# RMS factors applied to the results of two dense products, tokens turned unscaled in quarters, with a new layer front and new routing arithmetic

## The chip, the cores and the metric

The kernel runs on 1 core of one Trainium2 chip. The metric is the device time of one execution in microseconds (us), lower is better.

## The reference

256 tokens of width 1024 go through two blocks. Cut to what matters here:

```python
def hybrid_layer(x, ...):                                  # block 1, one layer
    z = rms_norm(x, g_mix) @ w_in
    ...
    merged = gt[:, :, 0] * (o_a @ p_a) + gt[:, :, 1] * (o_b @ p_b) + gt[:, :, 2] * (o_c @ p_c)
    x = x + merged @ w_out
    u = rms_norm(x, g_ffn) @ w_gu                          # 1024 -> 2 x 2816
    gate, up = jnp.split(u, 2, axis=-1)
    return x + (jax.nn.silu(gate) * up) @ w_down

def first_block(x, ...):
    ...
    return rms_norm(x, g_final)

def second_block(x, w_in, ...):                            # two layers
    for l in range(DEPTH_2):
        h = jnp.einsum('bsd,dc->bsc', x, w_in[l])
        a_q, a_k, a_v, b_q, b_k, b_v, i_q, i_k, i_w, c_q, c_kv, c_kr = split_cols(h)
        o_a = sliding_window_sink_attn(...)
        o_b = indexer_sparse_attn(...)                     # top 64 keys by sum_h w_idx * relu(q_idx k_idx)
        q_c = rms_norm_2(c_q, c_q_norm_g[l]) @ w_uq[l]
        kv_c = rms_norm_2(c_kv, c_kv_norm_g[l]) @ w_ukv[l]
        o_c = mla_attn(...)
        x = layer_norm(DEEPNORM_ALPHA * x + mix @ w_out[l], ln1_g[l], ln1_b[l])
        x = layer_norm(DEEPNORM_ALPHA * x + moe_ffn(x, ...), ln2_g[l], ln2_b[l])

def moe_ffn(x, ...):                                       # 16 experts in 4 groups
    scores = jax.nn.sigmoid(xt @ w_router)
    biased = (scores + router_bias).reshape(N, N_GROUPS, EXPERTS_PER_GROUP)
    group_score = jnp.sum(lax.top_k(biased, TOP_K)[0], axis=-1)
    g_sel = jnp.argmax(group_score, axis=-1)
    in_group = jnp.take_along_axis(biased, g_sel[:, None, None], axis=1)[:, 0]
    _, local = lax.top_k(in_group, TOP_K)
    ...
```

## The kernel before

**Data.** The tokens lie in `x_tok[128, t, 1024]` (t = 0, 1, 128 tokens each). For a product they are turned to `act_hi`/`act_lo` (`act_both`): 8 tiles k of 128 columns by 256 tokens. Every product is made from split operands: a number is rounded to a short form (hi) and its rest (lo), and three matmuls hi·hi, hi·lo, lo·hi stand for one (`three`, L966 to L968; in an FFN tile `both_tile`, L1106 to L1110, where hi and lo of the tokens are one 512-column operand). Weights come by DMA into `raw` in tiles of 128x2048; ScalarE writes their hi half `whi` (`split_hi`, L1757), VectorE their rest `wlo` (`split_lo`, L2194), and tile n lies in slot n % 3 of each. Five engine programs are written out by hand, one after the other, and semaphores tie them: the order of the code is the order of each engine.

**Dense part.** After w_out (4 tiles from number `T_WO`, each a `down_tile` of 24 matmuls) comes the FFN norm, then 11 FFN steps (`experts`): gate tile, up tile, w_down tile, from number `T_FFN` = 40. Of each step VectorE sums the two halves of gate and up (L2422), ScalarE makes silu (L1952), VectorE the product (L2442), ScalarE and VectorE its hi and lo. The norms before the FFN and after it (`g_final`) are one function each side: VectorE adds the product to x (`add`, L2386), ScalarE sums squares (L1808), GpSimd raises to the power -1/2 (L839), VectorE makes a diagonal matrix of the factors (`diag2`, L2395), TensorE turns and scales in one matmul x_tok · diag2 (`turn_scaled`, L1093), ScalarE and VectorE apply the gain by column while they round (L1815, L2410). While that runs TensorE does `keep_warm` matmuls (L1045), whose results nobody reads. The first tile is taken up column tile by column tile (`first_tile`).

**Layers of block 2.** `L_PAIRS` are column groups of w_in_2 that are made token half by token half, each from two weight tiles: pair 0 holds the indexer's columns, pair 1 those of the two low-rank vectors c_q and c_kv, pair 2 the window attention's queries. Then come two single column tiles (`columns`), the low-rank products (`up_queries`, `up_keys`), and the turned queries and keys. The indexer: GpSimd rotates its queries and keys (rope, L906 to L909, copies L917), TensorE turns them (L1352) and multiplies (L1411), ScalarE takes relu (L2047, L2048), VectorE sums the heads (L2532), strikes out the 64 largest in 8 rounds (L2539, L2540) and writes the mask (L2557, L2559). Weight splits lie between the rounds. After the mask the attention units begin with `logits` (L2223). The mean squares of c_q and c_kv are VectorE's (`norm_stats`, L2492 to L2496), the power GpSimd's (L930), the scaling VectorE's (L2521).

**Routing.** After the first layer norm TensorE turns the tokens, multiplies with the router (L1483), ScalarE makes exp (L2108), and VectorE finds each token's group out of 4 by pairwise comparison (L2636 to L2665, semaphore `one_ready`). TensorE counts tokens of each group (L1543 to L1546), VectorE orders the groups (L2668 to L2672, `ord_ready`; SyncE reads that order and issues the experts' weights, L743) and makes a 0/1 matrix of places (L2683, `put_ready`) with which TensorE gathers the tokens (L1558, L1559). `xt_hi`/`xt_lo` (L2105, L2629) are the split tokens it gathers from. `keep_warm` stands in TensorE's two waits.

In the profile before, `arena`, `small` and `pbuf` are the buffers from which the smaller tiles are carved.

## Time and profile before

| | |
|---|---|
| median of 3 runs | 1106.47 us (1105.86 to 1106.81) |
| the profiled execution | 1107.15 us, its span 1105.4 us |
| mean granted TensorE clock | 0.997 |
| TensorE busy | 1069.6 us, 97 % of the span |
| VectorE busy | 739.3 us, 67 % |
| ScalarE busy | 546.2 us, 49 % |
| GpSimd busy | 107.8 us, 10 % |

Times in the rows are us from the start of the span. A timeline row gives start, length, engine, line, operation, tiles, and in brackets the idle time before it with what ended it. A matmul's length contains its way through the array (0.39 us for 512 columns, though the next begins 0.23 us later), so lengths of matmuls are read from start to start.

### The profile page before, as it was taken

What the parts mean: (1) busy time and instruction counts of PE and PEld (TensorE: products, weight loads), DVE (VectorE), ACT (ScalarE), POOL (GpSimd) and SP (SyncE); (2) the same over time, 40 slices, a digit from 0 to 9 for tenths busy, and PEclk for the clock granted to TensorE, in tenths of its full rate; (3) what the DMA queues carried; (4) which work ended last, traced back from release to release, by engine and by line L of the source; (5) the groups of instructions that cost most, each with busy time, mean ns of one, the idle gap of its engine ahead of it and who ended that gap; (6) DMA issues with size and microseconds to landing.
All of it is one profiled execution on the core that took longest, in us unless ns stands there. A gap on an engine that the chain in (4) does not pass through costs nothing.

```text
span 1105.4 us, 15299 instructions
## 1 busy us (share of the span) xinstructions
PE 1069.6 (97%) x5828; PEld 872.7 (79%) x5828; DVE 739.3 (67%) x984; ACT 546.2 (49%) x728; POOL 107.8 (10%) x159
## 2 busy tenths in 40 slices
PE   8999999999999999999899999999998999999996
PEld 8899987888888888888787766777787877667765
DVE  5544635687576666659978745886879768357856
ACT  5344455673444444454753434664356625245741
POOL 3000020100000000015600000000067000000000
PEclk9999999999999999999999999999999999999998
DMA  9763443544465555534311878987344017789971
GB/s 293 222 207 115 127 157 128 180 165 151 152 219 194 192 180 195 186 116 134 114 61 39 312 277 337 369 322 265 119 141 150 5 49 274 271 319 374 348 266 39
DMA packets 107759, 214.59 MB, mean 194 GB/s; under 512 B 6834, under 2 KB 52042, under 8 KB 107696
## 3 DMA queue, kind: packets, MB, share of 16 engines
q1 hardware_dynamic: 105072, 209.38, 54.6%
q0 software_dynamic: 1312, 3.88, 1.1%
q8 instruction: 41, 0.67, 0.3%
q10 hardware_dynamic: 1312, 0.49, 0.2%
q14 instruction: 22, 0.18, 0.0%
HBM read 212.63 MB, written 1.09 MB: 193 GB/s over the span
## 4 chain that ended last, share of the span: by engine, by line
PE 75%; DVE 14%; ACT 4%; DMA 3%; issue 2%; POOL 1%; SPq 1%; ACTq 0%; DVEq 0%
PE ps L966 15%; PE ps L968 14%; PE ps L967 14%; PE ps L1107 7%; DVE wlo L2194 3%; PE ps L1106 3%; PE ps L1071 3%; PE ps L1622 2%; PE ps L1002 2%; PE ps L1004 2%; PE ps L1003 2%; ACT whi L1757 2%; DMA arena<-in_w_down 2%; PE ps L1037 2%; PE ps L1056 1%
## 5 line engine op out<-in xcount | busy, mean ns | idle before, releaser
L2194 DVE TENSOR_TENSOR wlo<-raw,whi 128x2048 fp32r<-128x2048 f32 (+4 forms) x145 | 316.0, 2181 | 180.7 <-ACT whi L1757 180.0
L1757 ACT ACTIVATE whi<-raw 128x2048 fp32r<-128x2048 f32 (+4 forms) x145 | 261.7, 1808 | 174.3 <-PE ps L968 71.7
L966 PE MATMUL ps<-whi,act_both 128*128 128x512 f32 (+2 forms) x416 | 155.4, 373 | 4.8 <-DVE wlo L2194 4.2
L968 PE MATMUL ps<-whi,act_both 128*128 128x512 f32 (+2 forms) x416 | 151.7, 365 | 0.0
L967 PE MATMUL ps<-wlo,act_both 128*128 128x512 f32 (+2 forms) x416 | 151.6, 364 | 0.0
L1107 PE MATMUL ps<-act_both,whi 128*128 128x512 f32 x344 | 119.1, 396 | 0.6 <-DVE wlo L2194 0.6
L2194 DVE TENSOR_TENSOR wlo<-arena,whi 128x2048 fp32r<-128x2048 f32 (+1 forms) x36 | 75.9, 2113 | 39.1 <-ACT whi L1757 39.0
L966 PE MATMUL ps<-whi,mix_hi 128*128 128x512 f32 (+1 forms) x244 | 96.0, 394 | 1.3 <-DVE mix_lo L2568 0.5
L966 PEld LDWEIGHTS ps<-whi,act_both 128*128 128x128 f32 x416 | 78.4, 188 | 22.9 <-issue 7.6
L968 PE MATMUL ps<-whi,mix_lo 128*128 128x512 f32 (+1 forms) x244 | 95.0, 389 | 0.0
L967 PE MATMUL ps<-wlo,mix_hi 128*128 128x512 f32 (+1 forms) x244 | 94.8, 389 | 0.0
L968 PEld LDWEIGHTS ps<-whi,act_both 128*128 128x128 f32 x416 | 78.4, 188 | 12.4
L967 PEld LDWEIGHTS ps<-wlo,act_both 128*128 128x128 f32 x416 | 78.5, 189 | 10.9
L1757 ACT ACTIVATE whi<-arena 128x2048 fp32r<-128x2048 f32 (+1 forms) x36 | 64.1, 1781 | 45.7 <-DMA arena<-in_w_up 24.7
L1106 PE MATMUL ps<-act_both,wlo 128*128 128x256 f32 x301 | 83.9, 279 | 0.0
L839 POOL TENSOR_TENSOR small<-small 128x1 f32<-128x1 f32 x14 | 8.2, 587 | 769.8 <-DVE small L2206 488.5
L1107 PEld LDWEIGHTS ps<-act_both,whi 128*128 128x128 f32 x344 | 62.2, 188 | 12.9 <-issue 0.9
L966 PE MATMUL ps<-act_both,whi 128*128 128x256 f32 x216 | 62.0, 287 | 0.0
L967 PE MATMUL ps<-act_both,whi 128*128 128x256 f32 x216 | 61.1, 283 | 0.0
L968 PE MATMUL ps<-act_both,wlo 128*128 128x256 f32 x216 | 61.1, 283 | 0.0
L1106 PEld LDWEIGHTS ps<-act_both,wlo 128*128 128x128 f32 x301 | 56.8, 189 | 1.9
L966 PEld LDWEIGHTS ps<-whi,mix_hi 128*128 128x128 f32 x244 | 45.8, 188 | 13.5 <-issue 2.9
(329 smaller groups left out, 1934.3 us busy)
## 6 DMA issues: line engine op xcount, KB each, us to landing
raw<-in_w_in SPq DMA_DIRECT2D x43, 1024.0 KB, 5.4
raw<-in_w_down SPq DMA_DIRECT2D x23, 1024.0 KB, 5.2
raw<-in_w_gu SPq DMA_DIRECT2D x22, 1024.0 KB, 5.1
raw<-in_w_out SPq DMA_DIRECT2D x12, 1024.0 KB, 4.9
raw<-in_w_gate SPq DMA_DIRECT2D x24, 512.0 KB, 5.6
raw<-in_w_up SPq DMA_DIRECT2D x24, 512.0 KB, 6.6
arena<-in_w_gate SPq DMA_DIRECT2D x20, 512.0 KB, 5.1
arena<-in_w_up SPq DMA_DIRECT2D x20, 512.0 KB, 6.2
```

What stands on the lines that cost most here:

```text
L966: pe.matmul(o, ah, bh, start=first, stop=False)
L967: pe.matmul(o, ah, bl, start=False, stop=False)
L968: return pe.matmul(o, al, bh, start=False, stop=last)
L1002: pe.matmul(o, a, cc, start=f, stop=False)
L1003: pe.matmul(o, a, d, start=False, stop=False)
L1004: x = pe.matmul(o, b, cc, start=False, stop=g)
L1037: x = pe.matmul(o[:, i, :], u["q"][i], u["k"][i], start=True, stop=True)
L1071: x = pe.matmul(oo, pt[:, b * P:(b + 1) * P], u["v"][i][kt], start=f, stop=g)
L1106: pe.matmul(ps[:, bank + part, 0:256], wl[:, k, m], act_hi[:, k, :], start=False, stop=False)
L1107: x = pe.matmul(ps[:, bank + part, :].rearrange("p (a b) -> p a b", a=2), wh[:, k, m], act_both[:, k, :, :], start=k == 0, stop=k == KD - 1)
L1757: act.activation(whi[:, c % 3, 0:n], raw_of(c, v)[:, 0:n], ACT.Copy).then_inc(hi_made, 1)
L2194: dve.tensor_tensor(wlo[:, c % 3, 0:n], raw_of(c, v)[:, 0:n], whi[:, c % 3, 0:n].bitcast(F32), ALU.subtract)\
```

## The change

**Both dense norms.** x is turned as it is, in four quarters (`turn_early`: four transposes of 128x128), between the parts of the last w_out tile, of the first gate tile (`first_gate`), of the last w_down tile and of layer 0's first columns. ScalarE (`early_rounded`) and VectorE (`remainders`) apply only the gain by column. The factor rstd of each token is applied afterwards: in the FFN to the gate sums (`normed`, one VectorE multiply of 128x512 in each of 11 steps with `rstd_rows`, a tile that TensorE and VectorE make once), to the result of w_down where it is added to x, and in layer 0 as the scale of the evacuations. (The up sums are left unscaled, since the factor comes in at that addition.) `turn_scaled` and the two `keep_warm(0, 6)` are gone; ScalarE's splits of the second FFN step stand ahead of the first silu.

**Layer front, both layers.** The indexer's rope is VectorE's (`idx_rope`), its turns and products on TensorE stand ahead in the order, the mean squares and the scaling of c_q and c_kv are ScalarE's (`c_squares`), the addition of eps GpSimd's, their gains are applied by column when the turned values are split (three narrow operations each on ScalarE and VectorE), and weight splits 6 to 9 and the strike rounds are regrouped on VectorE.

**Routing, both layers.** Fewer VectorE operations between exp and the orders and places, counts and keys multiplied by 4, the key made by a matmul on a constant, `max_index` in place of copy and mask; half of `xt_lo` moved behind `put_ready`; the second `xt_hi` moved behind exp; the router's second half for t = 0 moved behind the turn of t = 1; `keep_warm` 2 to 0, 12 to 6 and 10 to 6.

```diff
+                rows(0, 0).then_inc(early_out, 1)
+                rows(0, 1).then_inc(early_out, 1)
+                turn_early(last, 0, 0)
+                rows(1, 0).then_inc(early_out, 1)
+                turn_early(last, 0, 1)
+                if last == 1:
+                    rows(1, 1, (0,))
+                    turn_early(last, 1, 0)
+                    rows(1, 1, (1,)).then_inc(tile_used, 1)
+                else:
+                    rows(1, 1).then_inc(tile_used, 1)
+            def turn_early(nth, t, half):
+                pe.wait_ge(x_added, 4 * nth - 4 + 2 * t + half + 1)
+                for k in range(4 * half, 4 * half + 4):
+                    x = pe.transpose(early_at(t, k), x_tok[:, t, k * P:(k + 1) * P], ident)
+                x.then_inc(early_full, 1)
...
-                for k in range(KD):
-                    o = turned_at(k, slice(t * P, (t + 1) * P), apart)
-                    x = pe.matmul(o, x_tok[:, t, k * P:(k + 1) * P], diag2[:, t, :], start=True, stop=True)
...
+                rounded(0)
+                turn_early(1, 1, 1)
+                rounded(1)
...
+                        for t in range(TT):
+                            pe.wait_ge(diag_set, TT + t + 1)
+                            x = pe.matmul(ps[:, 4, t * P:(t + 1) * P], cst[:, C_FOUR:C_FOUR + P], diag2[:, t, :], start=True, stop=True)
+                        x.then_inc(rows_full, 1)
+                        both_tile(c + 1, v, 2, (1,))
...
-                    keep_warm(0, 6)
-                    for t in range(TT):
-                        pe.wait_ge(diag_set, 2 * TT + t + 1)
-                        turn_scaled(t, True, True)
...
+                            elif half == 0:
+                                turn_early(2, 1, 0)
+                                turn_early(2, 1, 1)
...
-                for half in range(2):
-                    for t in range(TT):
-                        pair_columns(1, half, t)
-                pe.wait_ge(rope_done, l * 5 + 1)
+                pair_columns(1, 0, 0)
+                pair_columns(1, 0, 1)
+                pe.wait_ge(idx_turned, l + 1)
                 turns(pairs(IQ, 2) + doubled(0))
-                pair_columns(2, 0, 0)
+                pair_columns(1, 1, 0)
                 tb_wait(1)
...
-                for half in range(2):
-                    pe.wait_ge(tr_lo, l * 12 + 5 + half)
-                    route(0, half, (0, 1, 2))
+                pe.wait_ge(tr_lo, l * 12 + 5)
+                route(0, 0, (0, 1, 2))
                 keep_warm(5, 4)
                 turn(x_tok, 1, l * 8, True)
-                keep_warm(5, 2)
+                pe.wait_ge(tr_lo, l * 12 + 6)
+                route(0, 1, (0, 1, 2))
                 for half in range(2):
...
-                keep_warm(7, 12)
+                keep_warm(7, 6)
...
-                keep_warm(7, 10)
+                keep_warm(7, 6)
...
+            def early_rounded(nth, t):
+                for half in range(2):
+                    act.wait_ge(early_full, 4 * nth - 4 + 2 * t + half + 1)
+                    for k in range(4 * half, 4 * half + 4):
+                        act.activation(act_hi[:, k, t * P:(t + 1) * P], early_at(t, k), ACT.Copy,
+                                       scale=g_col[:, nth * KD + k:nth * KD + k + 1]).then_inc(early_hi, 1)
...
+                def c_squares(t):
+                    for q, (c0, n) in enumerate(((CQ, C_QR), (CKV, C_KVR))):
+                        x = act.activation(c_squared[q], h[:, t, c0:c0 + n], ACT.Square, scale=n ** -0.5,
+                                           accum_out=cvar[:, 2 * t + q:2 * t + q + 1])
+                    return x
...
+                    if nth == 1:
+                        dve.tensor_tensor(x, x, o, ALU.add).then_inc(x_added, 1)
+                    else:
+                        dve.scalar_tensor_tensor(out=x, in0=o, scalar=rstd[:, t:t + 1], in1=x, op0=ALU.mult, op1=ALU.add).then_inc(x_added, 1)
+                def remainders(t, half):
+                    for k in range(4 * half, 4 * half + 4):
+                        dve.wait_ge(early_hi, 2 * KD * (nth - 1) + KD * t + early_shared(t, k) + 1)
+                        m = slice(t * P, (t + 1) * P)
+                        dve.scalar_tensor_tensor(out=act_lo[:, k, m], in0=early_at(t, k), scalar=g_col[:, nth * KD + k:nth * KD + k + 1],
+                                                 in1=act_hi[:, k, m].bitcast(F32), op0=ALU.mult, op1=ALU.subtract).then_inc(early_lo, 1)
...
+                def normed(e):
+                    dve.wait_ge(gate_sum, e + 1)
+                    g = f_gate.rearrange("p (a b) -> p a b", a=2)
+                    dve.tensor_tensor(g, g, spread(rstd_rows, 1, 2), ALU.mult).then_inc(gate_ready, 1)
...
+                    dve.tensor_tensor(a3, x, c3, ALU.mult)
+                    dve.tensor_tensor(b3[:, :, 0:32], x[:, :, 32:64], s_lo, ALU.mult)
+                    lk(dve.tensor_tensor(b3[:, :, 32:64], x[:, :, 0:32], s_hi, ALU.mult))
+                    lk(dve.tensor_tensor(x, a3, b3, ALU.add))
...
+                dve.tensor_copy(key_sb, keys)
+                lk(dve.max(sorted_key, keys))
+                dve.max_index(vec8, sorted_key, key_sb).then_inc(ord_ready, 1)
```

TensorE at the end of w_out and the start of the FFN, before: the six fillers, sixteen scaled turns, then the first gate tile.

```order
L1045 MATMUL ps<-mix_hi 128x512 x6
L1093 MATMUL ps<-arena,x_tok 128x128 x16
L1123 MATMUL ps<-act_both,whi 128x256 x8
L1126 MATMUL ps<-act_both,wlo 128x256 x8
L1130 MATMUL ps<-act_both,whi 128x256 x8
```

The same place of the change (L971 to L973 are w_out's last tile, L1029 the transposes, L1160 and L1161 `first_gate`):

```order
L973 MATMUL ps<-whi,act_both 128x512
L1029 MATMUL ps<-cst,x_tok 128x128 x4
L971 MATMUL ps<-whi,act_both 128x512
L972 MATMUL ps<-wlo,act_both 128x512
L973 MATMUL ps<-whi,act_both 128x512
L1029 MATMUL ps<-cst,x_tok 128x128 x4
L971 MATMUL ps<-whi,act_both 128x512
L972 MATMUL ps<-wlo,act_both 128x512
L973 MATMUL ps<-whi,act_both 128x512
L1160 MATMUL ps<-act_both,whi 128x256
L1161 MATMUL ps<-act_both,wlo 128x256
```

Fillers and scaled turns are gone, and turns stand among the products.

VectorE in a layer's front, before: the last of four norm statistics, the indexer's weights (L2513), a weight split, the scaling of c_q and c_kv, then the indexer's sums (L2532).

```order
L2492 BN_STATS small<-arena 128x6
L2493 BN_AGGR small<-small 128x2
L2494 SCALAR_TENSOR_TENSOR small<-small 128x1
L2496 TENSOR_SCALAR small<-small 128x1
L2513 TENSOR_SCALAR small<-arena 128x4 x2
L2515 TENSOR_SCALAR small<-small 128x8
L2194 TENSOR_TENSOR wlo<-raw,whi 128x768
L2521 SCALAR_TENSOR_TENSOR arena<-arena,small 128x256
L2521 SCALAR_TENSOR_TENSOR arena<-arena,small 128x128
L2521 SCALAR_TENSOR_TENSOR arena<-arena,small 128x256
L2521 SCALAR_TENSOR_TENSOR arena<-arena,small 128x128
L2532 SCALAR_TENSOR_TENSOR arena<-pbuf,small,cst 128x256
```

The same place of the change (L2270 is `split_lo`, L2589 to L2600 the indexer's rope, L2615 its sums):

```order
L2270 TENSOR_TENSOR wlo<-raw,whi 128x1424
L2589 TENSOR_TENSOR arena<-arena,cst 128x320
L2590 TENSOR_TENSOR arena<-arena,cst 128x5x32
L2591 TENSOR_TENSOR arena<-arena,cst 128x5x32
L2592 TENSOR_TENSOR arena<-arena 128x320
L2599 COPY arena<-arena 128x128
L2600 COPY arena<-arena 128x128
L2270 TENSOR_TENSOR wlo<-raw,whi 128x2048 x2
L2606 TENSOR_SCALAR small<-arena 128x4 x2
L2608 TENSOR_SCALAR small<-small 128x8
L2615 SCALAR_TENSOR_TENSOR arena<-pbuf,small,cst 128x256
```

Statistics, scaling and the 768-column split no longer stand ahead of the sums; the rope does, among the splits.

VectorE in the routing, before, from the end of the group comparison to the places:

```order
L2650 TENSOR_TENSOR arena<-arena 128x32
L2653 TENSOR_REDUCE arena<-arena 128x8
L2665 TENSOR_SCALAR arena<-arena 128x8
L2629 TENSOR_TENSOR mix_lo<-x_tok,mix_hi 128x512
L2668 SCALAR_TENSOR_TENSOR arena<-ps,cst 128x8
L2670 MAX arena<-arena 128x8
L2671 CAST arena<-arena 128x8
L2672 TENSOR_SCALAR arena<-arena 128x8
L2674 TENSOR_TENSOR arena<-arena 128x16
L2675 TENSOR_REDUCE arena<-arena 128x4
L2676 SCALAR_TENSOR_TENSOR arena<-arena 128x4
L2678 SCALAR_TENSOR_TENSOR arena<-arena,ps 128x8
```

The same place of the change:

```order
L2730 TENSOR_TENSOR arena<-arena,cst 128x32
L2733 TENSOR_REDUCE arena<-arena 128x8
L2713 TENSOR_TENSOR mix_lo<-x_tok,mix_hi 128x512
L2747 COPY arena<-ps 128x8
L2748 MAX arena<-ps 128x8
L2749 MAX_INDEX arena<-arena 128x8
L2750 TENSOR_TENSOR arena<-arena 128x16
L2751 TENSOR_REDUCE arena<-arena 128x4
L2753 SCALAR_TENSOR_TENSOR arena<-arena,ps 128x8
```

Three operations of this piece are gone, and `MAX_INDEX` is new; ahead of it, 11 operations between the biased scores and `one_ready` (L2658 to L2665) have become 8.

## Rows read from the trace of the kernel before

**Rows 1.** The page: busy time, share of the span, instructions of TensorE

```profile
PE 1069.6 (97%) x5828; PEld 872.7 (79%) x5828; DVE 739.3 (67%) x984; ACT 546.2 (49%) x728; POOL 107.8 (10%) x159
```

**Rows 2.** Windows: length, busy PE, PEld, DVE, ACT, POOL, PEclk, DMA share, GB/s

```profile
306.00:472.00 166.00, 165.92 (x879) 142.30 (x880) 111.33 (x74) 68.68 (x51) 0.00 (x0) 1.00 0.59 194
...
495.00:540.00 45.00, 42.70 (x272) 37.40 (x272) 39.57 (x96) 26.41 (x31) 31.31 (x47) 1.00 0.43 139
...
595.00:617.00 22.00, 18.91 (x134) 15.74 (x133) 19.32 (x51) 9.74 (x14) 0.55 (x1) 1.00 0.36 109
```

**Rows 3.** Timeline of TensorE from w_out to the second FFN step

```profile
286.53 1.52 PE L1045 MATMUL ps<-mix_hi 128*128 128x512 f32 x6
288.96 3.84 PE L1093 MATMUL ps<-arena,x_tok 128*128 128x128 f32 x32 [0.92 <-DVE arena L2395]
292.56 1.01 PE L1123 MATMUL ps<-act_both,whi 128*128 128x256 f32 x3
...
306.08 0.47 PE L1107 MATMUL ps<-act_both,whi 128*128 128x512 f32 x1 [0.61 <-DVE wlo L2194]
```

**Rows 4.** Timeline of VectorE in the last FFN steps

```profile
451.79 0.69 DVE L2442 TENSOR_TENSOR arena<-arena 128x512 f32<-128x512 f32 x1
...
463.57 2.29 DVE L2194 TENSOR_TENSOR wlo<-raw,whi 128x2048 fp32r<-128x2048 f32 x1 [0.79 <-ACT whi L1757]
```

**Rows 5.** Timeline of TensorE from w_down to pair 1 of layer 0

```profile
477.84 1.52 PE L1045 MATMUL ps<-mix_hi 128*128 128x512 f32 x6
...
483.85 0.48 PE L966 MATMUL ps<-whi,act_both 128*128 128x512 f32 x1
...
494.87 0.32 PE L966 MATMUL ps<-whi,act_both 128*128 128x356 f32 x1
```

**Rows 6.** Timeline of VectorE in layer 0's front

```profile
503.39 0.43 DVE L2492 BATCH_NORM_STATS2 small<-arena 128x6 f32<-128x256 f32 x1
...
508.82 1.41 DVE L2521 SCALAR_TENSOR_TENSOR arena<-arena,small 128x256 f32<-128x256 f32 x4
510.15 0.86 DVE L2532 SCALAR_TENSOR_TENSOR arena<-pbuf,small,cst 128x256 f32<-128x256 f32 x2
...
537.39 0.68 DVE L2223 SCALAR_TENSOR_TENSOR pbuf<-ps,cst 128x512 f32<-128x512 f32 x1
```

**Rows 7.** Timeline of ScalarE in layer 0's front

```profile
495.07 0.60 ACT L2012 ACTIVATE arena<-ps 128x512 f32<-128x512 f32 x1 [1.26 <-PE ps L968]
...
499.03 1.92 ACT L1757 ACTIVATE whi<-raw 128x2048 fp32r<-128x2048 f32 x1 [1.57 <-PE ps L968]
...
507.81 1.03 ACT L2047 ACTIVATE pbuf<-ps 128x1024 f32<-128x1024 f32 x1 [2.96 <-PE ps L1411]
```

**Rows 8.** Timelines of layer 1's front: TensorE (pair 1 begins), VectorE (first logits)

```profile
802.76 0.32 PE L966 MATMUL ps<-whi,act_both 128*128 128x356 f32 x1
...
846.52 0.68 DVE L2223 SCALAR_TENSOR_TENSOR pbuf<-ps,cst 128x512 f32<-128x512 f32 x1
```

**Rows 9.** Waits of TensorE: released by; us in total, times, longest us

```profile
PE ps L966 <- DVE wlo L2194: 4.5, 6, 1.8
```

**Rows 10.** Timeline of GpSimd in layer 0's front

```profile
495.81 0.89 POOL L906 TENSOR_TENSOR arena<-arena,cst 128x320 f32<-128x320 f32 x1 [2.63 <-ACT arena L2012]
...
497.75 2.80 POOL L909 TENSOR_TENSOR arena<-arena 128x320 f32<-128x320 f32 x1
```

**Rows 11.** Timelines of layer 0's routing: ScalarE, VectorE, SyncE's queue

```profile
602.55 2.08 ACT L2105 ACTIVATE mix_hi<-x_tok 128x1024 fp32r<-128x1024 f32 x1
...
603.29 1.98 DVE L2629 TENSOR_TENSOR mix_lo<-x_tok,mix_hi 128x1024 fp32r<-128x1024 f32 x1
...
609.54 0.17 DVE L2672 TENSOR_SCALAR arena<-arena 128x8 int32<-128x8 int32 x1
...
610.95 0.75 DVE L2683 TENSOR_SCALAR moe_r<-cst,arena 128x384 fp32r<-128x384 f32 x2
...
610.75 0.35 SPq L743 DMA_DIRECT2D raw<-in_w_gate  x1
```

More of the change, by code:

```diff
@@ L604, in apart, with early_at, early_shared @@
                 eng.wait_ge(semaphore, awaited)
-        def turned_at(k, m, apart):
-            if apart and m.start:
-                return ps[:, 6 + k // 4, (k % 4) * P:(k % 4 + 1) * P]
-            return ps[:, 2 + k // 2, (k % 2) * S + m.start:(k % 2) * S + m.stop]
+        def early_at(t, k):
+            bank = EARLY_BANK[t][k]
+            c = EARLY_BANK[t][:k].count(bank) * P
+            return ps[:, bank, c:c + P]
+        def early_shared(t, k):
+            return max(x for x in range(KD) if EARLY_BANK[t][x] == EARLY_BANK[t][k])
         def unit_first(u):
@@ L987, in cols_tile, with down_tile @@
                     last.then_inc(tile_used, 1)
-            def down_tile(c, v, hi, lo, first, last):
+            def down_tile(c, v, hi, lo, first, last=0):
                 tile_ready(c, v)
@@ L994, in down_tile, with rows @@
                 wl = wlo[:, s, :].rearrange("p (k c) -> p k c", k=2)
-                for t in range(TT):
-                    for half in range(2):
-                        for k in range(2):
-                            m, n = slice(t * P, (t + 1) * P), slice(half * 512, half * 512 + 512)
-                            o = ps[:, 4 + 2 * t + half, :]
-                            f, g = first and k == 0, last and k == 1
-                            a, b, cc, d = hi[:, k, m], lo[:, k, m], wh[:, k, n], wl[:, k, n]
-                            pe.matmul(o, a, cc, start=f, stop=False)
-                            pe.matmul(o, a, d, start=False, stop=False)
-                            x = pe.matmul(o, b, cc, start=False, stop=g)
-                        if last and not (t and half):
-                            x.then_inc(early_out, 1)
-                x.then_inc(tile_used, 1)
+                def rows(t, half, ks=(0, 1)):
+                    m, n = slice(t * P, (t + 1) * P), slice(half * 512, half * 512 + 512)
+                    for k in ks:
+                        x = three(ps[:, 4 + 2 * t + half, :], hi[:, k, m], lo[:, k, m], wh[:, k, n], wl[:, k, n],
+                                  first and k == 0, last > 0 and k == 1)
+                    return x
+                if not last:
+                    for t in range(TT):
+                        for half in range(2):
+                            x = rows(t, half)
+                    x.then_inc(tile_used, 1)
+                    return
+                rows(0, 0).then_inc(early_out, 1)
[14 more added lines that the diff above has]
+                x.then_inc(early_full, 1)
             def turn(src, t, before, by_four=False, first_bank=0, halves=(0, 1)):
@@ L1125, in first_tile @@
                 for k in range(KD):
-                    pe.matmul(o, wl[:, k, m], act_hi[:, k, :], start=False, stop=apart and k == KD - 1)
+                    pe.matmul(o, wl[:, k, m], act_hi[:, k, :], start=False, stop=False)
                 for k in range(KD):
                     if k % 2 == 0:
-                        pe.wait_ge(k_lo, pairs + k // 2 + 1)
-                    pe.matmul(ps[:, 0, 256:512] if apart else o, wh[:, k, m], act_lo[:, k, :], start=apart and k == 0, stop=k == KD - 1)
@@ L2378, in _, with early_sums @@
                                       act_hi[:, 4 * half:4 * half + 4, :].bitcast(F32), ALU.subtract).then_inc(m_lo, 1)
-            for n in range(T_WO + 2, T_FFN + 2):
+            for n in range(T_WO + 2, T_FFN + 1):
                 split_lo(n)
-            def add_and_factor(used, nth):
+            def early_sums(used, nth, rest):
                 def add(t, half):
@@ L2448, in experts @@
                 gate(0, c0, v0)
+                for t in range(TT):
+                    dve.wait_ge(rstd_ready, TT + t + 1)
+                    dve.tensor_scalar(diag2[:, t, :], ident, rstd[:, t:t + 1], 0.25, ALU.mult, ALU.mult).then_inc(diag_set, 1)
                 split_lo(c0 + 2, v0)
+                dve.wait_ge(rows_full, 1)
+                dve.tensor_copy(rstd_rows, ps[:, 4, 0:S]).then_inc(rows_set, 1)
+                dve.wait_ge(rows_set, 1)
+                normed(0)
                 product(0, c0 + 1, v0)
@@ L2618, in layer @@
                     else:
-                        for part in range(2):
-                            turned_lo_half(l * 3 + 1, 0, part)
+                        turned_lo_half(l * 3 + 1, 0, 0)
                     dve.wait_ge(gln_in, l * 64 + 32)
@@ L2684, in layer @@
                 ins.then_inc(put_ready, 1)
-                rest_of(1, slice(1, 2))
-                dve.tensor_scalar(inside, pos, float(S), None, ALU.is_lt)
-                beaten(flat(bi), 8)
-                ranks(8, cnt8)
+                for t in range(TT):
+                    rest_of(t, slice(1, 2))
+                dve.tensor_scalar(inside, pos, 4.0 * S, None, ALU.is_lt)
+                beaten(flat(bi), 8, ALU.is_gt)
+                lk(over(8, cnt8, ALU.add))
                 def gates():
```

346 lines of the change are left out of this document (179 added, 167 removed).

## The prediction, written before the change was run

> **What bounds the kernel.** I read the page first: TensorE is busy for 97 % of the span [rows 1]. The windows by stage say where the missing 3 % lie: an FFN step has none (165.9 us busy in 166), while a layer's front (42.7 of 45 us) and a routing (18.9 of 22) do, and the clock is granted in full in all of them [rows 2]. But busy is not useful: the timelines show filler matmuls, and the stretches from the last product before a norm to the first one behind it, which no busy share reveals [rows 3, 5]. So the time is that of TensorE's useful matmuls plus such stretches, and only what shortens a stretch counts. In a front VectorE is the other bound: 39.6 us busy of 45 [rows 2], and the first `logits` wait for its chain of sums, strikes and mask [rows 6].
>
> **FFN entry.** w_out's last matmul gives way to the fillers at 286.53; the first gate matmul starts at 292.56, the second step's gate at 306.08 [rows 3]. That is 19.55 us. What useful work lies in it? From 306.08 to the fillers at 477.84 [rows 3, 5] lie ten steps and one w_down tile. A matmul of 512 columns takes 0.227 us from one to the next (six fillers in 1.52 us, less one way through the array), a w_down tile of 24 therefore 5.45; so a step takes (171.76 - 5.45)/10 = 16.63, and gate plus up 11.18. The change needs besides: 16 transposes at 0.112 each (the 32 passes of L1093 take 3.6 us up to the gate matmul; I take a transpose as one pass) = 1.8, and two matmuls for `rstd_rows`, 0.45. 13.4 in all, a gain of 6.1. I take off 0.5 for waits: turned quarters must be added, rounded and given their remainders in time, and the fourth is turned only 0.9 us after w_out's end while VectorE still has four remainders and an addition of 0.7 us to do. **5.6 us.** ScalarE's reordered splits should take the wait of 0.61 for `wlo` away; its cover is the up tile.
>
> **FFN steps.** `normed` adds one 128x512 multiply per step, 0.69 us by its like, L2442 [rows 4], and silu waits for it. VectorE is busy 111.3 of 166 us [rows 2], 11.1 of 16.6 per step, and behind the gate sum it stands idle for 0.79 us until the next split is ready [rows 4]: the multiply fits there. What is late next is silu, by 0.7 us; the hidden values are used a whole tile later (5.6 us). I cost it at nothing; with the cover gone it is at most 11 times 0.69, 7.6 us.
>
> **Layer 0 entry.** Fillers begin at 477.84, pair 0 at 483.85 [rows 5]: 6.0 us. The change puts 1.8 us of transposes there: 4.2, of which I keep **4.1 us**. The scaled evacuations replace unscaled ones of the same size; the two more at the single columns lie beside TensorE's work.
>
> What do both entries do to the clock? It was granted in full where TensorE waited in a routing for 3 of 22 us [rows 2], so I cost the new mixture at nothing. A rule speaks against that. The Trainium skill, "TensorE: Matmul & The Clock Gate", Part 4, says that a transpose does not count as TensorE's busy time for the clock, and the change puts transposes where fillers and real matmuls stood. By that rule the clock could be low behind each entry; no row here shows transposes at a fallen clock. What it would cost I work out as rival 3, from rows.
>
> **Layer fronts.** Count from X, the end of pair 0 (494.87 [rows 5], 802.76 [rows 8]). Before, layer 0's sums start at X+15.3 and logits at X+42.5 [rows 6]; layer 1's logits at X+43.8 [rows 8]. Removed from VectorE ahead of the sums are the four statistics (from 503.39, 4.1 us) and the scaling (1.41) [rows 6]; added are two ropes, 1.6 us each by 128x512 at 0.69 scaled to 320 columns with their fixed part, which fall mostly in waits for ScalarE's splits. Now ScalarE decides: behind X it has an evacuation (0.60), split 4 (1.92), the turned queries, split 5, an evacuation, two squares, and relu (1.03 and a half of that) [rows 7], about 9 us of work and 1.7 of waits for TensorE: sums at X+10.7, 4.6 earlier. Given back: split 6 (0.96 us, 768 columns at the rate of the others) moves behind them, and the remainder of the low-rank vectors is three operations instead of one (+0.4): 3.2 by VectorE's way. ScalarE's way to the first exp gives some 2.2. I take **2.8 us** in layer 0 and, since layer 1 is 1.3 us slower at the same point and loses that to a rope wait and a `wlo` wait of the same chain, **3.9 us** there. The largest wait of TensorE for `wlo`, 1.8 us [rows 9], should go too, but it is no further gain: logits wait for VectorE.
>
> One row speaks against the move: on GpSimd a rope's last addition, 320 columns, took 2.80 us while VectorE made a split, and its first multiply of that width 0.89 us while VectorE stood idle [rows 10]. If the hold is mutual, VectorE's new ropes pay for it too; but the two engines' ropes now lie apart in time, and GpSimd's statistic and small ropes beside them take 0.2 to 0.3 us a piece, so I cost it at nothing, at most 1 us per layer.
>
> **Routing, each layer.** Before: `xt_lo` holds VectorE from 603.29 for 1.98 us, `xt_hi` ScalarE to 604.6, and exp waits for that; the order is ready at 609.7, SyncE issues weights at 610.75, the places are written from 610.95 [rows 11]. Removed: half of `xt_lo` ahead of the comparison (0.9, of which I count 0.8, the exp behind `xt_hi` coming earlier too), three small operations at 0.17 to 0.2 ahead of `one_ready` (0.5), one in the ordering and one in the places (0.4). Added: `max_index`, which no row shows; nearest are operations of 0.17 on 8 columns [rows 11], so from 0.17 to twice that. Gather and weights shift together: **1.7 us**, twice, 3.4. The fillers taken out here (14 of 24) leave TensorE idle instead, at no cost but the clock's.
>
> **Sum.** 5.6 + 4.1 + 2.8 + 3.9 + 3.4 = 19.8 us, 1.8 %. The profiled execution took 1107.15, so 1087.35; the median of the runs stands 0.68 under it: **1086.7 us**. A measurement tells 0.2 %, 2.2 us, from no change.
>
> **The rivals.**
> 1. *The fronts give nothing*: ScalarE, with squares, scalings and three narrow roundings more, is late for relu or the first exp. For it: it decides already by my count. Against: 26.4 busy of 45 us [rows 2]. 1086.7 + 6.7 = 1093.4. Chance 0.13.
> 2. *The entries give half*: TensorE waits at each quarter for addition, rounding, remainder. For it: each quarter passes three engines; against, half a tile of matmuls lies between. 1086.7 + 4.9 = 1091.6. Chance 0.08.
> 3. *The clock falls* from 2.4 to 1.2 GHz, in the thinned routings or behind the entries. Against: a wait of 1.8 us [rows 9] and routings with waits had it at 1.00 [rows 2]. One tile of 5.6 us at half speed behind each entry adds 11.2: 1097.9; the 5 us between places and the end of a routing [rows 2, 11], twice, 1096.7. Say 1097. Chance 0.04.
> 4. *It does not do what it says*: the stretches stay, held by something unseen: 1106.5. Chance 0.02.
> 5. *Slower*: the FFN step becomes a chain (gate sum, `normed`, silu, product, hidden split, w_down) longer than TensorE's 16.63. It must exceed it by 2.0 us in ten steps to eat 19.8; at 3 us the time is 1086.7 + 30 = 1117. For it: one operation more in that chain, between two splits of 2.29 us that can hold VectorE. Against: a third of VectorE's step is idle. Chance 0.03.
>
> The forecast itself has 0.70; its own range is 1083.5 to 1090.5 (transposes and waits at nothing, layer 0's front at 3.2, layer 1's at 4.3, against `max_index` at twice, waits doubled and 2.2 for layer 0). To leave out no more than 2 in 10 the range goes from 1082 to 1094.5, over rivals 1 and 2. Faster 0.95, same 0.02, slower 0.03.
>
> **What would show it.** In the profile after: no matmul L1045 at the norms; the first gate matmul at about 288 and the second step's at 300.5; 16.6 us per FFN step as before; pair 0 begins right behind w_down; X to logits about 39.7 us in both layers, with VectorE without idle before them; the order to SyncE about 1.7 us earlier after the router; PEclk at 1.00 everywhere. Wrong would be: gaps of over 0.5 us at L1160 or L1029; FFN steps over 16.7 us; logits released by ScalarE; a low clock in a routing.

## The result

The change is faster, by 1.35 %: 1091.78 us median of 4 executions (1089.31 to 1094.59) against 1106.64 of before, a ratio of 0.9865 with a 95 % interval from 0.9846 to 0.9883. The forecast was 1086.7, with a range from 1082 to 1094.5: the sign is right, the gain is 14.9 us where 19.8 were forecast. The profiled execution took 1093.08 us, its span 1091.3.

The page of the changed kernel; its third row is the TensorE clock in 40 slices, in tenths:

```profile
PE 1060.8 (97%) x5768; PEld 865.7 (79%) x5768; DVE 744.5 (68%) x976; ACT 554.5 (51%) x766; POOL 93.5 (9%) x141
...
PEclk9999999999999999999899999999999999999998
```

TensorE is as busy as before by share [rows 1]; in us its busy time is 8.8 less. One slice in the middle has an 8; before no stretch of the kernel's middle had one. It comes back below.

Timeline of TensorE in the changed kernel, from w_out's last matmul over the turn between the first gate's parts to the second FFN step (the second matmul of the 300.02 row), then layer 0's entry and the first matmul of pair 1 in each layer:

```profile
287.79 0.40 PE L973 MATMUL ps<-whi,act_both 128*128 128x512 f32 x1
288.05 0.35 PE L1160 MATMUL ps<-act_both,whi 128*128 128x256 f32 x1
...
300.02 0.62 PE L1122 MATMUL ps<-act_both,whi 128*128 128x512 f32 x2
...
475.63 1.03 PE L1029 MATMUL ps<-cst,x_tok 128*128 128x128 f32 x8
...
484.70 0.32 PE L971 MATMUL ps<-whi,act_both 128*128 128x356 f32 x1
...
793.61 0.32 PE L971 MATMUL ps<-whi,act_both 128*128 128x356 f32 x1
```

The gate follows w_out after 0.26 us, and the second step starts at 300.25 instead of 306.08 [rows 3]: 5.8 us. Pair 1 starts at 484.70 instead of 494.87 [rows 5], 10.2 earlier, so layer 0's entry gave 4.3. Eight transposes take 0.79 us from start to start, 0.1 each.

Timeline of VectorE in an FFN step of the changed kernel (L2517 is `normed`), then its first logits in layers 0 and 1:

```profile
455.69 1.23 DVE L2503 TENSOR_REDUCE arena<-ps 128x512 f32<-128x1024 f32 x1 [0.77 <-PE ps L1122]
456.95 0.69 DVE L2517 TENSOR_TENSOR arena<-arena 128x512 f32<-128x512 f32 x1
457.70 2.29 DVE L2270 TENSOR_TENSOR wlo<-raw,whi 128x2048 fp32r<-128x2048 f32 x1
...
525.91 0.69 DVE L2299 SCALAR_TENSOR_TENSOR pbuf<-ps,cst 128x512 f32<-128x512 f32 x1 [0.45 <-PE ps L1052]
...
834.52 0.69 DVE L2299 SCALAR_TENSOR_TENSOR pbuf<-ps,cst 128x512 f32<-128x512 f32 x1 [0.31 <-PE ps L1052]
```

The multiply stands exactly in the hole of [rows 4], and from the second to the last step the gate sums lie 16.48 us apart, against 16.54 before. The logits now come 41.2 us after X in layer 0 and 40.9 in layer 1, against 42.5 and 43.8 [rows 5 to 8]: gains of 1.3 and 2.9, and VectorE now waits just before them (0.45 and 0.31 us), which it did not.

The windows of the changed kernel around the slice with the lower clock (same columns as [rows 2]):

```profile
528.00:531.00 3.00, 2.55 (x16) 1.30 (x16) 2.90 (x6) 2.18 (x9) 2.84 (x5) 1.00 0.60 244
531.00:534.00 3.00, 2.00 (x13) 1.46 (x13) 2.86 (x6) 3.00 (x13) 2.10 (x5) 0.81 0.00 0
534.00:537.00 3.00, 3.00 (x18) 2.66 (x18) 1.13 (x7) 1.66 (x6) 0.00 (x0) 0.50 0.00 0
537.00:540.00 3.00, 3.00 (x16) 2.95 (x16) 1.70 (x4) 1.15 (x4) 0.00 (x0) 0.55 0.02 5
```

For some 7 us TensorE runs at 1.2 GHz, behind a stretch at the first attention units in which it was idle for 1.5 of 6 us. The last of these waits, 1.00 us for an evacuation by ScalarE (L2078), ends at 532.51, and the matmuls that start then are the first slow ones. The same wait stands at the same place in the trace of before, where the clock did not fall (TensorE):

```profile
543.91 0.64 PE L1352 MATMUL ps<-cst,arena 128*96 128x128 f32 x4 [1.00 <-ACT arena L2024]
```

Routing of layer 0 in the changed kernel: VectorE's order and places, SyncE's first weight issue, ScalarE's split waiting for the weights, the first expert product:

```profile
599.99 0.16 DVE L2749 FIND_INDEX8 arena<-arena 128x8 uint32<-128x8 f32 x1
...
601.06 0.75 DVE L2758 TENSOR_SCALAR moe_r<-cst,arena 128x384 fp32r<-128x384 f32 x2
...
601.19 0.35 SPq L749 DMA_DIRECT2D raw<-in_w_gate  x1
...
605.26 1.06 ACT L1805 ACTIVATE whi<-raw 128x1024 fp32r<-128x1024 f32 x1 [1.41 <-DMA raw<-in_w_up]
...
607.63 0.49 PE L971 MATMUL ps<-whi,act_both 128*128 128x512 f32 x1 [0.80 <-DVE wlo L2270]
```

The issue now comes 0.13 us behind the places; before, it came 0.20 ahead of them [rows 11]. The order gained less than the places, and the first expert product waits for the weights, which hang on the order.

### The profile page after: what moved, and what is told of

Same layout as the page of the kernel before. It is cut to its first block, busy times and chain, and to the rows that moved or that the text cites. A ratio compares the mean times of both kernels' runs of the same rounds, so it can differ in the third digit from the quotient of the medians.

```text
span 1091.3 us, 15196 instructions
## 1 busy us (share of the span) xinstructions
PE 1060.8 (97%) x5768; PEld 865.7 (79%) x5768; DVE 744.5 (68%) x976; ACT 554.5 (51%) x766; POOL 93.5 (9%) x141
## 4 chain that ended last, share of the span: by engine, by line
PE 85%; DVE 7%; POOL 3%; ACT 3%; issue 1%; DMA 1%; SPq 0%; ACTq 0%; DVEq 0%; POOLq 0%
PE ps L971 19%; PE ps L973 18%; PE ps L972 18%; PE ps L1122 7%; PE ps L1121 3%; PE ps L1094 3%; PE ps L1670 2%; PE ps L1060 2%; PE ps L1079 2%; PE ps L1692 1%; PE ps L1052 1%; DVE x_tok L2679 1%; ACT whi L1805 1%; DVE x_tok L2677 1%; POOL arena L915 1%
## 5 line engine op out<-in xcount | busy, mean ns | idle before, releaser
L2270 DVE TENSOR_TENSOR wlo<-raw,whi 128x2048 fp32r<-128x2048 f32 (+4 forms) x145 | 316.6, 2186 | 160.7 <-ACT whi L1805 160.0
L971 PE MATMUL ps<-whi,act_both 128*128 128x512 f32 (+2 forms) x448 | 168.2, 376 | 1.8 <-DVE wlo L2270 1.6
L973 PE MATMUL ps<-whi,act_both 128*128 128x512 f32 (+2 forms) x448 | 164.2, 367 | 0.0
L972 PE MATMUL ps<-wlo,act_both 128*128 128x512 f32 (+2 forms) x448 | 164.1, 366 | 0.0
L971 PE MATMUL ps<-whi,mix_hi 128*128 128x512 f32 x332 | 130.5, 393 | 1.4 <-DVE mix_lo L2652 0.5
L973 PE MATMUL ps<-whi,mix_lo 128*128 128x512 f32 x332 | 129.2, 389 | 0.0
L972 PE MATMUL ps<-wlo,mix_hi 128*128 128x512 f32 x332 | 129.1, 389 | 0.0
L971 PEld LDWEIGHTS ps<-whi,act_both 128*128 128x128 f32 x448 | 84.4, 188 | 20.7 <-issue 5.4
L2270 DVE TENSOR_TENSOR wlo<-arena,whi 128x2048 fp32r<-128x2048 f32 (+1 forms) x36 | 76.0, 2113 | 34.0 <-ACT whi L1805 34.0
L973 PEld LDWEIGHTS ps<-whi,act_both 128*128 128x128 f32 x448 | 84.4, 188 | 13.6
L1805 ACT ACTIVATE whi<-arena 128x2048 fp32r<-128x2048 f32 (+1 forms) x36 | 64.1, 1781 | 42.5 <-DMA arena<-in_w_up 25.1
L971 PEld LDWEIGHTS ps<-whi,mix_hi 128*128 128x128 f32 x332 | 62.3, 188 | 17.0 <-issue 4.1
L973 PEld LDWEIGHTS ps<-whi,mix_lo 128*128 128x128 f32 x332 | 62.3, 188 | 13.2
L972 PEld LDWEIGHTS ps<-wlo,mix_hi 128*128 128x128 f32 x332 | 62.4, 188 | 12.5
L971 PE MATMUL ps<-act_both,whi 128*128 128x256 f32 x216 | 62.0, 287 | 0.0
L973 PE MATMUL ps<-act_both,wlo 128*128 128x256 f32 x216 | 61.1, 283 | 0.0
```

The source lines that it names most:

```text
L971: pe.matmul(o, ah, bh, start=first, stop=False)
L972: pe.matmul(o, ah, bl, start=False, stop=False)
L973: return pe.matmul(o, al, bh, start=False, stop=last)
L1805: act.activation(whi[:, c % 3, 0:n], raw_of(c, v)[:, 0:n], ACT.Copy).then_inc(hi_made, 1)
L2270: dve.tensor_tensor(wlo[:, c % 3, 0:n], raw_of(c, v)[:, 0:n], whi[:, c % 3, 0:n].bitcast(F32), ALU.subtract)\
```

## The experiments

Each was run beside executions of before on the same chip. Over all these runs before took 1106.39 us in 37 of 48 executions at a mean clock of 0.997 or more (the median of these), and 1108.7 to 1110.4 in the other 11, at 0.994 or 0.995. Below, "full clock" means the executions at 0.997 or more.

**1. The three parts alone, and the change once more.** `dense_only`, `front_only` and `routing_only` are before with one group of the diff's hunks each; in `dense_only` the rows are made with ones and a factor of 1 instead of 4 and 0.25, since those constants belong to the routing.

```diff
-cst[:, C_FOUR:C_FOUR + P], diag2[:, t, :]
+cst[:, C_ONE:C_ONE + P], diag2[:, t, :]
-dve.tensor_scalar(diag2[:, t, :], ident, rstd[:, t:t + 1], 0.25, ALU.mult, ALU.mult)
+dve.tensor_scalar(diag2[:, t, :], ident, rstd[:, t:t + 1], None, ALU.mult)
```

> Only the two dense norms are changed; layer front and routing are those of before. Theory (the parts add up as the trace of the change shows them: 5.8 us at the FFN entry, 4.4 at layer 0's): 1106.6 - 10.2 = 1096.4 us, and the FFN steps stay at 16.6 us. Rival (the FFN steps give part of it back through the added multiply): over 1099 us.

> Only the layer fronts are changed. Theory (TensorE's own work becomes the bound at the first logits, so the front gives 1.3 us in layer 0 and 2.9 in layer 1, of which 0.7 is lost behind it): 1106.6 - 3.5 = 1103.1 us. If the clock falls in layer 0's attention units because of the new front, some executions stand 3.2 us above that. Rival (my prediction's sizes, 2.8 and 3.9): 1099.9 us.

> Only the routing is changed. Theory (1.6 us earlier at the places, but the first expert product only 1.2 and 1.4 earlier): 1106.6 - 2.6 = 1104.0 us. Rival (prediction: 1.7 each): 1103.2. Rival (fewer fillers bring the clock down): above 1106.

> The changed kernel, once more. Theory (a stretch of 7 us at 1.2 GHz at the start of layer 0's attention units in some executions, not in others): the times fall in two groups about 3 to 4 us apart, 1089 to 1090.5 with a mean clock of 0.997 or more, and 1093 to 1094.6 with 0.994. Rival (plain scatter): clocks and times unrelated.

| kernel | median, us | ratio, interval | full clock: median, executions | lower clock |
|---|---|---|---|---|
| dense_only | 1098.21 | 0.9917 [0.9894, 0.9941] | 1097.50, 3 of 4 | 1100.66 |
| front_only | 1104.05 | 0.9972 [0.9959, 0.9986] | 1103.24, 6 of 10 | 1105.4 to 1106.1 |
| routing_only | 1105.86 | 0.9991 [0.9980, 1.0003] | 1105.28, 7 of 10 | 1107.2 to 1107.4 |
| after_again | 1090.92 | 0.9864 [0.9840, 0.9888] | 1090.36, 3 of 5 | 1093.12, 1094.29 |

At full clock the parts give 8.9, 3.2 and 1.1 us, together 13.2, the whole 16.0. Two of the three theories for the parts were too high: `dense_only` by 1.3 us (10.2 were expected), `routing_only` by 1.5 (2.6). The parts are not additive: in the dense part alone the logits of layer 0 still hang on before's VectorE chain (the row has no wait ahead of it), and come 43.9 us after its pair 1 began, 1.4 later than before, so 1.4 of the 10 us won at the entries was given back there. Timelines of TensorE (pair 1) and VectorE (logits) in `dense_only`:

```profile
484.95 0.32 PE L974 MATMUL ps<-whi,act_both 128*128 128x356 f32 x1
...
528.87 0.68 DVE L2278 SCALAR_TENSOR_TENSOR pbuf<-ps,cst 128x512 f32<-128x512 f32 x1
```

The trace of `routing_only` shows the like in layer 1: the first expert product of layer 0 stands 2.2 us earlier than before (614.92 against 617.07), pair 1 of layer 1 1.4 (801.32), its first logits only 0.5. These are its rows of TensorE and VectorE:

```profile
801.32 0.32 PE L963 MATMUL ps<-whi,act_both 128*128 128x356 f32 x1
...
845.97 0.68 DVE L2224 SCALAR_TENSOR_TENSOR pbuf<-ps,cst 128x512 f32<-128x512 f32 x1
```

From pair 1 to the logits took 44.7 us there, 43.8 before. With the new front it takes 41 us in every trace but that of `pool_rope` (experiment 4). The two losses, 1.4 and 0.9 us, would make up most of the 2.8 by which the parts fall short of the whole; each is read from one execution. The front alone gave 3.2, as its theory said (3.5) and not as I predicted (6.7). The routing alone can't be told from nothing by its interval.

The changed kernel shows two groups, by time and clock together: over both sets five executions from 1089.3 to 1090.9 at full clock and four from 1093.1 to 1094.6 at 0.994 or 0.995. The plain-scatter rival falls: the profile of `after_again`, an execution at 0.997, has the same stretch without the fall.

```profile
531.00:534.00 3.00, 1.86 (x15) 1.30 (x15) 2.86 (x7) 2.88 (x10) 2.43 (x6) 1.00 0.00 0
534.00:537.00 3.00, 3.00 (x32) 2.81 (x30) 2.79 (x8) 2.90 (x11) 0.00 (x0) 1.00 0.02 5
```

The same order with the same idle time thus runs at either clock. Before has such executions too (11 of 48), and the lower group costs 3.1 us there, 3.3 here.

Where the clock fell is known only of profiled executions; of the change's four with a lowered clock that is one. The one profile of `dense_only` has the fall in layer 0's units, that of `front_only` in layer 1's, again right behind the wait of 1.00 us (TensorE, then the window):

```profile
849.20 0.77 PE L1352 MATMUL ps<-cst,arena 128*96 128x128 f32 x4 [1.00 <-ACT arena L2025]
...
852.00:855.00 3.00, 3.00 (x18) 2.62 (x18) 1.92 (x5) 2.00 (x7) 0.00 (x0) 0.50 0.00 0
```

**2. Fillers around the first units.** `no_fill` drops the fillers ahead of the first unit's products, `units_warm` adds six at units 2 and 3, `warm_nofill` does both, in both layers:

```diff
                 tb_wait(2)
-                keep_warm(3, 4)
...
+                    if i == 3:
+                        pe.wait_ge(pt_ready, nu + 1)
+                        keep_warm(2, 4)
                     late_turns(i)
+                    if i == 2:
+                        keep_warm(2, 2)
```

> The changed kernel with six more fillers in each layer's attention units (two at unit 2, four at unit 3 of each layer, where TensorE stands idle for 0.3 to 1.0 us). Theory (thin work at the first units lets the clock fall to 1.2 GHz in some executions, 3 to 4 us each): no execution with a mean clock under 0.996, all of them between 1089 and 1091.5. Rival (the fall comes from what stands ahead of the units, or from elsewhere): the upper group stays in about half of the executions, and the fillers cost up to 1 us.

> The changed kernel without the four fillers ahead of the first unit's products in each layer (0.9 us of TensorE). Theory (the first logits now wait for TensorE, by 0.45 and 0.31 us): 0.3 to 0.8 us less than the changed kernel in undisturbed executions, 1089.6 to 1090. Rival (VectorE is the bound): the same 1090.4. If thin work ahead of the units brings the clock down, falls become more frequent than 4 of 9.

> Both edits: no fillers ahead of the first unit, six more at units 2 and 3. Theory: the best of the set, 1089 to 1090.5 in all executions. Rival (the fillers ahead of the first unit hold the clock up): executions at 1093 and more remain.

`units_warm` 1093.62 (0.9874 [0.9856, 0.9893]), `no_fill` 1090.45 (0.9846 [0.9831, 0.9861]), `warm_nofill` 1093.86 (0.9869 [0.9850, 0.9887]). `units_warm` was a bad test, and its timeline of TensorE says why:

```profile
532.94 1.21 PE L1068 MATMUL ps<-mix_hi 128*128 128x512 f32 x4 [1.48 <-ACT pt L1840]
```

The fillers' bank had to be freed by ScalarE first, so they stood behind the idle time, made it longer (1.48 instead of 1.00 us) and delayed the units by 1.35 us in layer 0. Twice that is what its two executions at full clock lost (1092.92 and 1093.34 against 1090.36). The clock fell in the profiled execution too, in layer 1, and in that of `warm_nofill` in layer 0; two of four executions of each were at 0.994 to 0.996. So both theories missed, and whether fillers that wait for nothing guard the clock stayed open. `no_fill` saved nothing (full clock 1090.45 in 5 of 5, against 1090.36): my expectation that TensorE's amount of work delays the logits is wrong. No execution of it had a lowered clock. Its timelines of TensorE, ScalarE and VectorE:

```profile
524.08 0.38 PE L1397 MATMUL ps<-cst,arena 128*128 128x128 f32 x2
525.49 0.70 PE L1052 MATMUL ps<-arena 64*128 64x256 f32 x4 [1.03 <-ACT arena L2077]
...
524.28 0.84 ACT L2067 ACTIVATE arena<-ps,small 128x256 f32<-128x256 f32 x2 [2.25 <-PE ps L973]
525.00 0.39 ACT L2077 ACTIVATE arena<-ps 128x256 f32<-128x256 f32 x1
...
526.23 0.69 DVE L2298 SCALAR_TENSOR_TENSOR pbuf<-ps,cst 128x512 f32<-128x512 f32 x1 [0.49 <-PE ps L1052]
```

The chain is: second single column tile on TensorE, its evacuation on ScalarE (two scaled operations in layer 0, 0.84 us), then that of the last turned keys, then the first products, then the logits. Where the fillers stood, TensorE now waits for ScalarE.

**3. The cover of the added multiply.** `normed4` does it four times in each step, so the gate is scaled by the factor's fourth power.

```diff
+                    for i in range(3):
+                        dve.tensor_tensor(g, g, spread(rstd_rows, 1, 2), ALU.mult).then_inc(scaled_some, 1)
+                        dve.wait_ge(scaled_some, 3 * e + (i + 1))
                     dve.tensor_tensor(g, g, spread(rstd_rows, 1, 2), ALU.mult).then_inc(gate_ready, 1)
```

> The changed kernel with the multiply of the gate sums done four times in each FFN step (the gate is scaled by the fourth power of the factor, so its output differs), some 2.3 us more in the chain gate sum, silu, product, hidden of each of the 11 steps. Theory (the added multiply lies in idle time of VectorE, 11.1 of 16.6 us busy): at most 3 us more, an FFN step stays under 16.8. Rival (the chain is near its limit): 11 times up to 2.3 us more, about 1115.

1091.33 us (0.985 [0.9834, 0.9867]), all four executions at full clock: 1.0 more than the change's full-clock median, for 33 multiplies more. One multiply per step is free; three more cost at most 0.1 us a step. In the traces the last step's gate sum starts at 456.02 us, against 455.98 in `after_again`, and pair 1 of layer 0 0.45 later: the steps hide the three, what stands behind the last one does not.

**4. The indexer's rope back on GpSimd,** everything else as changed:

```diff
+                rope(5, 64, C_CC, C_SS, cols(IQ, 5), 1, [(0, IK)], 1)
...
-                pe.wait_ge(idx_turned, l + 1)
+                pe.wait_ge(rope_done, l * 5 + 1)
...
-                idx_rope(0)
...
-                idx_rope(1)
```

> The changed kernel with the indexer's rope back on GpSimd, all else as changed. Theory (TensorE's order now asks for the turned queries 3.8 us after pair 0, and GpSimd's rope of one half took 4.8 us): TensorE waits 2 to 3 us before the indexer's turns, sums and logits come that much later, 2 to 5 us more in all, 1092.5 to 1095.5. Rival (the move was worth nothing, since other work fills in): 1090.4.

1099.81 us (0.9931 [0.9915, 0.9946]), 9.4 more than the change at full clock, none of the 6 executions at full clock. TensorE's timeline, and its windows:

```profile
491.70 1.54 PE L1399 MATMUL ps<-cst,arena 128*128 128x128 f32 x6 [2.90 <-POOL arena L923]
```

```profile
489.00:492.00 3.00, 0.30 (x2) 0.31 (x3) 0.74 (x1) 0.00 (x0) 2.50 (x4) 0.93 0.32 59
492.00:495.00 3.00, 3.00 (x13) 3.00 (x12) 0.00 (x0) 1.72 (x3) 0.00 (x0) 0.51 0.83 290
```

TensorE waits 2.9 us for the rope in layer 0 and 2.8 in layer 1, which is what the theory priced, and behind both waits the clock falls to 1.2 GHz, which no expectation had; so the loss is twice the theory's 2 to 5 us. The profiled execution was the slowest of the six (1104.29), with a third fall at layer 1's units. So the early turns of the indexer work only because the rope is VectorE's.

**5. The two remedies mended.** `swap_evac` exchanges the two ScalarE steps that experiment 2 showed in the chain; `fill7` puts fillers into a bank nobody reads then; `swap_fill7` does both.

```diff
-                evac_single(1)
                 block_out(3, [(one(ak_t), 0, 2)], 6)
+                evac_single(1)
...
+                    if i in (2, 3):
+                        keep_warm(7, 4 if i == 3 else 1)
                     late_turns(i)
```

> The changed kernel with five fillers per layer (one at unit 2, four at unit 3) in a bank nobody reads then, so that they wait for nothing and lie inside TensorE's idle time of 1.0 us at unit 3. Theory (thin work at the first units brings the clock down): no execution with a mean clock under 0.996; undisturbed ones at 1089.3 to 1091, as the changed kernel. Rival (the fall depends on something else): executions at 1093 and more remain, about 4 in 10.

> The changed kernel with two ScalarE steps exchanged ahead of the attention units: the evacuation of the last turned keys before that of the second single column tile. Theory (the first logits wait neither for TensorE's amount of work nor for VectorE, but for ScalarE, which evacuates the column tile first): logits up to 0.45 us earlier in layer 0 and 0.31 in layer 1, 0.5 to 0.8 us less in all. Rival (TensorE's amount of work bounds it): no change.

> Both last edits in the changed kernel: the two ScalarE steps exchanged, and five fillers per layer at units 2 and 3 that wait for nothing. Theory (the exchange is worth 0.1 us and the fillers nothing in undisturbed executions, and they guard the clock): 1090.3 us, all executions at a mean clock of 0.996 or more and under 1092. Rival (whether the clock falls there has nothing to do with the fillers): one to three of the executions at 1093 and more.

`fill7` 1090.48 (0.985 [0.9835, 0.9865]), `swap_evac` 1090.44 (0.985 [0.9835, 0.9866]), `swap_fill7` 1090.36 (0.9855 [0.9838, 0.9871]). The exchange brought the logits of layer 0 only 0.1 us forward, where up to 0.45 was expected: VectorE still waited 0.32 us for the products, which now stand behind the four fillers of `keep_warm(3, 4)`, as its timelines of TensorE and ScalarE show:

```profile
524.29 1.17 PE L1068 MATMUL ps<-mix_hi 128*128 128x512 f32 x4
525.39 0.70 PE L1052 MATMUL ps<-arena 64*128 64x256 f32 x4
...
524.58 0.39 ACT L2078 ACTIVATE arena<-ps 128x256 f32<-128x256 f32 x1 [2.43 <-PE ps L1397]
```

The keys are out at 525.0, the fillers until 525.4. Exchange and `no_fill` together would take both away; by my estimate, from VectorE's waits of 0.32 and 0.33 us, for 0.3 us at most per layer. That was not tried. The new fillers of `fill7` cost nothing where they wait for nothing. No execution of the three, 14 in all, had a lowered clock, but neither had those of `no_fill` and `normed4`, 9 more without new fillers. Before's own executions beside these had it in 6 of 27, so the chips can do it. Against 4 of 9 of the change, 0 of 23 suggests that small shifts in time matter; it does not show that the fillers do. None of these versions is measurably faster than the change at full clock.

## Why the prediction was right in its sign and too high in its gain

**Entries: right.** 5.8 and 4.3 us for 5.6 and 4.1. A transpose counts as one pass; the feared wait at the fourth quarter didn't come, since the gate follows w_out at once. The small excess is part of the 0.5 taken off for waits, and transposes of 0.10 us instead of 0.112.

**FFN steps: right.** `normed` lies in VectorE's idle time, and `normed4` shows room for four.

**Layer fronts: the step that failed.** The terms of 2.8 and 3.9 us measured 1.3 and 2.9, and behind layer 1's logits another 0.8 was lost (56.8 us from there to the router's turns in `after_again`, 56.0 before). The first half of the step held: layer 0's sums begin 10.2 us after X, where 10.7 were forecast and 15.3 stood before. What failed is the way from the sums to the logits. I counted 1.4 us given back there, and 3.8 were, as `after_again` shows (VectorE, then ScalarE):

```profile
495.23 0.87 DVE L2615 SCALAR_TENSOR_TENSOR arena<-pbuf,small,cst 128x256 f32<-128x256 f32 x2 [0.23 <-ACT pbuf L2110]
...
505.87 1.27 DVE L2631 SCALAR_TENSOR_TENSOR mix_lo<-ps,arena,mix_hi 128x256 fp32r<-128x256 f32 x3 [1.01 <-ACT mix_hi L2126]
...
511.20 4.21 DVE L2270 TENSOR_TENSOR wlo<-raw,whi 128x512 fp32r<-128x512 f32 x2
...
500.81 1.50 ACT L2119 ACTIVATE arena<-arena,small 128x256 f32<-128x256 f32 x4 [3.32 <-POOL small L935]
```

Split 6 and the narrow operations cost what I had counted. Added to them are 1.0 us in which VectorE waits for ScalarE's rounding of the low-rank vectors (ScalarE's scaling had waited 3.3 us for GpSimd's power of the mean squares), 1.0 us more in two splits beside GpSimd's rope (4.21 us for both, 0.82 and 2.35 before; I had feared such a hold only for VectorE's new ropes, and costed it at nothing), and 0.4 us of waiting for the first products. That last wait is a second chain, over the column tile and ScalarE's evacuations; "It is no further gain: logits wait for VectorE" held for before, and I carried it over to the change. It ended 0.45 and 0.31 us behind VectorE's own chain, so it explains less than half of the shortfall. The move of the rope, costed at nothing, is what makes the front possible: 9.4 us without it, part of that by the clock. Rival 1 came nearest: ScalarE was late, though neither for relu nor for the first exp, and it cost part of 2.5 us instead of 6.7.

**Routing: mis-sized.** 1.7 us per layer was made of the places, which did gain that, though the removed operations alone added up to 1.7 and `max_index` was never taken off. The order for SyncE gained some 0.3 less, 1.4 (609.71 to 600.15, where the places went from 610.95 to 601.06) (`xt_lo` and the comparison count for both, the operation saved in the places doesn't), and the first expert product waits for the weights: it gained 1.4 and 1.5 us in `after_again`. `max_index` took 0.09 and 0.16 us, within its bounds. With before's front and norms the routing gave 1.1 us in all, of 3.4.

**The clock: rival 3, in another place.** I looked for it in the thinned routings and behind the entries; both ran at full clock in the profiles. In the profiled execution it fell at layer 0's first attention units; four of nine executions had a lowered clock, 3.3 us each, and of the other three no trace shows the place. It isn't new with the change: 11 of 48 executions of before had a lowered clock too, though where in them it fell no trace shows either. I had only three executions of before, none of them that slow; with the clocks of a dozen I would probably have had this term. The Trainium skill, "TensorE: Matmul & The Clock Gate", Part 4, says that a transpose does not count as busy in the way a product does, from which I took a risk at the entries; 16 transposes there, among products, did no harm in any profile taken. The stretch that fell does hold transposes and small products with idle time between them, which fits the rule but does not single it out.

In sum, against 19.8 forecast: entries +0.4, fronts -2.5, routings -0.5, and the clock's term, which is -1.4 in the first median. The rest, about 0.9 us, lies in stages that the change doesn't touch. In the `after_again` trace they lost 0.3 and 0.8 behind the first logits and 0.6 in layer 0's experts, and won 1.1 behind the first expert product of layer 1. The stretch from layer 0's first expert product to pair 1 of layer 1 took from 185.6 us (`front_only`) to 187.3 (`fill7`) in kernels that share its code, so differences of this size were not isolated.

Of my own range one end was not worked out: the terms named for 1090.5 add up to less than 2 us above 1086.7, not 3.8. With them alone the full-clock median of the change, 1090.36, would lie outside.

**Open:** what decides in a given execution whether the clock falls at the first units. The same order with the same idle times did both, and no experiment separated fillers from chance. The wait of 1.00 us ahead of it stands in before and in the change, and no version without it was run. Open is also what each of the delays between sums and logits is worth, since they are read from traces and only the last was tested (`no_fill`, `swap_evac`).

## What to carry to other kernels

A factor by row that only scales a product's result can be applied behind the product: the product then starts as soon as its operand is turned, and the multiply costs nothing where the engine has idle time in each step. When a chain is shortened at its start, follow it to its end: what the faster part then waits for, and the second-longest chain into the same instruction, down to single evacuations, set the gain. A part tried alone can show less than it is worth in the whole, when an older chain behind it gives its lead back. Read more than one execution's clock before and after, and give a stretch of small products with idle time a term of its own.

## What was unexpected of the hardware

- Idle time of 2.9 us on TensorE was followed by a stretch at 1.2 GHz (0.51 over 3 us) in the profiled `pool_rope`; waits of 1.0 us at the first units were followed by it in some executions and not in others of the same kernel.
- A small addition of GpSimd took 2.39 us for 128 columns at 523.67 in `no_fill`, beside a split of VectorE that ran from 523.44 for 2.30 us; its like took 0.46 at 521.80.

```profile
521.80 0.46 POOL L915 TENSOR_TENSOR arena<-arena 128x128 f32<-128x128 f32 x1
...
523.67 2.39 POOL L915 TENSOR_TENSOR arena<-arena 128x128 f32<-128x128 f32 x1
```

- VectorE's operations on two numbers per partition took 0.45 to 0.81 us beside an operation of GpSimd's rope and 0.16 between two of them (`no_fill`, L2306 and L2307).

```profile
530.02 0.16 DVE L2306 TENSOR_TENSOR small<-small 128x2 f32<-128x2 f32 x1
530.22 0.81 DVE L2307 TENSOR_TENSOR small<-small 128x2 f32<-128x2 f32 x1
```
